# Sample attention of a hybrid decoder step: eight samples stacked in the rows of one tile, probabilities as weights

## What is computed

```python
s_c = einsum('btgrd,bngd->btgrn', q, k_cmp) * SCALE + bias    # 15 compressed blocks
p_c = masked_softmax(s_c);  o_c = einsum('btgrn,bngd->btgrd', p_c, v_cmp)
s_s = einsum('btgrd,btgkd->btgrk', q, k_sel) * SCALE + bias   # 256 cached keys (two pages) + the new one
p_s = masked_softmax(s_s);  o_s = einsum('btgrk,btgkd->btgrd', p_s, v_sel)
s_w = einsum('btgrd,bkgd->btgrk', q, kw) * SCALE + bias       # 256 keys of the window + the new one
p_w = masked_softmax(s_w);  o_w = einsum('btgrk,bkgd->btgrd', p_w, vw)
return gates[..., 0:1] * o_c + gates[..., 1:2] * o_s + gates[..., 2:3] * o_w
```

## Time and profile before

| | |
|---|---|
| median of 3 executions | 2619.27 us (2617.09 to 2621.42) |
| the profiled execution | 2622.14 us, its span 2620.4 us |
| TensorE busy | 2496.6 us, 95% of the span |
| VectorE, ScalarE, GpSimd busy | 657.9, 381.8, 132.6 us |
| mean granted TensorE clock | 0.976 |
| DMA | 326.33 MB, mean 125 GB/s |

### The profile page before, as it was taken

The page is one execution under the profiler, slowest core; times in us unless marked ns, Lnnn a source line. Parts: engine busy times, 40 slices in busy tenths (PEclk is TensorE's granted clock), DMA queues, the critical chain, the costliest instruction groups (busy, mean ns, idle before and its releaser), DMA issues.

```text
span 2620.4 us, 40309 instructions
## 1 busy us (share of the span) xinstructions
PE 2496.6 (95%) x18046; PEld 2040.0 (78%) x18046; DVE 657.9 (25%) x1320; ACT 381.8 (15%) x1039; POOL 132.6 (5%) x233
## 2 busy tenths in 40 slices
PE   8999999999989899999899999999999998999995
PEld 7887887778877678888788778878788776788884
DVE  0131321216235220111211322212342452201112
ACT  0121111121025110000201111111110241100002
POOL 0000000010110110000000000000201101100000
PEclk9999999999999989999999999999999898899998
DMA  6532332346422333444343232323554223334442
GB/s 211 177 113 89 104 101 82 123 158 208 155 87 65 110 118 127 145 144 148 109 145 128 97 99 84 112 82 114 188 180 160 65 81 112 113 119 152 142 151 81
DMA packets 86779, 326.33 MB, mean 125 GB/s; under 512 B 11808, under 2 KB 11840, under 8 KB 84432
## 3 DMA queue, kind: packets, MB, share of 16 engines
q1 hardware_dynamic: 73152, 266.44, 31.2%
q0 software_dynamic: 13456, 57.33, 6.2%
HBM read 313.29 MB, written 18.82 MB: 127 GB/s over the span
## 4 chain that ended last, share of the span: by engine, by line
PE 91%; DVE 4%; ACT 3%; issue 1%; DMA 1%; POOL 0%; DVEq 0%; ACTq 0%; SPq 0%; POOLq 0%
PE PB L500 67%; PE PB L722 2%; PE PB L838 2%; PE PB L600 2%; PE PB L610 1%; PE PB L607 1%; PE PB L470 1%; ACT ARENA L886 1%; PE PB L569 1%; PE PB L582 1%; PE PB L771 1%; PE PB L859 1%; PE PB L817 1%; ACT ARENA L1101 1%; PE PB L877 1%
## 5 line engine op out<-in xcount | busy, mean ns | idle before, releaser
L500 PE MATMUL PB<-XT,WT 128*128 128x264 f32 (+1 forms) x6016 | 1438.2, 394 | 16.4 <-DMA WT<-in_w_all 7.0
L500 PEld LDWEIGHTS PB<-XT,WT 128*128 128x128 f32 (+1 forms) x6016 | 1125.3, 191 | 233.8 <-issue 25.4
L500 PE MATMUL PB<-H,WT 128*128 128x264 f32 x2048 | 456.5, 386 | 3.1 <-DVE H L1549 3.1
L500 PEld LDWEIGHTS PB<-H,WT 128*128 128x128 f32 x2048 | 389.0, 190 | 70.2 <-issue 3.8
L886 ACT ACTIVATE ARENA<-PB 128x128 f32<-128x128 f32 (+6 forms) x213 | 93.4, 454 | 386.7 <-PE PB L600 167.3
L1546 DVE SCALAR_TENSOR_TENSOR H<-H,PB 128x264 f32<-128x264 f32 x32 | 13.7, 430 | 303.6 <-PE PB L500 303.6
L1151 DVE COPY SHO<-PB 128x9 f32<-128x9 f32 x66 | 11.0, 167 | 310.1 <-ACT H L908 258.7
L383 POOL DMA_DIRECT2D out<-in_c_win x16 | 8.1, 509 | 1389.1 <-DVE ARENA L1295 1389.1
L1117 ACT ACTIVATE ARENA<-XT 128x1056 f32<-128x1056 f32 x8 | 8.7, 1083 | 458.5 <-DVE XT L1570 458.0
L908 ACT ACTIVATE H<-PB,PD 128x264 f32<-128x264 f32 x58 | 27.8, 479 | 299.2 <-PE PB L500 299.1
L1557 DVE SCALAR_TENSOR_TENSOR XT<-PB,XT 128x264 f32<-128x264 f32 x32 | 13.8, 433 | 207.0 <-PE PB L500 207.0
(11 more groups left out here) (275 smaller groups left out, 2079.4 us busy)
## 6 DMA issues: line engine op xcount, KB each, us to landing
WT<-in_w_all SPq DMA_DIRECT2D x504, 512.0 KB, 4.7
out<-in_c_win POOLq DMA_DIRECT2D x16, 512.0 KB, 5.4
ARENA<-in_c_cmp POOLq DMA_DIRECT2D x64, 128.0 KB, 4.3
ARENA<-in_c_sel POOLq DMA_DIRECT2D x64, 128.0 KB, 2.6
ARENA<-in_c_win POOLq DMA_DIRECT2D x32, 256.0 KB, 3.4
ARENA<-in_states POOLq DMA_DIRECT2D x4, 1024.0 KB, 8.8
out<-ARENA POOLq DMA_DIRECT2D x4, 1024.0 KB, 6.1
ARENA<-in_w1d POOLq DMA_DIRECT2D x4, 1024.0 KB, 5.1
```

What stands on the lines that cost most here:

```text
L500: ins = mm(PB[0:m, bank, 0:T], WT[:, s, k, 0:m], x, start=start, stop=stop)
```

## The change

The eight samples are done at once. A tile's partitions now hold a row for each head of each sample (16 heads x 8 samples = 128). Two neighbouring samples share a strip of 32 columns of the array, and four strips make the 128: sample b = 2m + odd is in strip m. The query weights `QZ` of a sample are 32 wide with the other sample's 16 columns zero, so that both samples of a strip add into the same PSUM rows. Matmuls of neighbouring m write to PSUM partitions 32m to 32m+31.

- Scores: first the four even samples, then the four odd ones, each 16 matmuls of 128x32 weights by 257 keys and 8 by 15 keys.
- Softmax once, over 128 partitions instead of 16.
- Seven transposes of up to 128x128 instead of 56 small ones; ScalarE copies them into `PTZ`, `PCZ` and `PNT`.
- Output: the probabilities (32 columns) are now the weights and 256 columns of values stream: 2 x (16 + 4) + 8 matmuls; two transposes turn the result back, and VectorE copies it into `H`.
- Compressed keys and values are read where they lie, without copies. The gates are picked into 128 partitions with 12 matmuls instead of 3.
- Two buffers hold the keys of four samples each, and then the values of the same four. Loads: keys of the even samples behind `cm_v out` (where the first two samples' loads stood); keys of the odd ones behind prompt units 5, 6 and 7; values of each half behind the scores of that half.
- Projection matmuls: 24, 44, 8 and 6 behind the steps, 82 in place of 128; the 46 others come in `project(L, "gates")`, which now stands ahead of the wait for `zb_v out`. `TZB` is computed after the attention.

```diff
-for sample in range(NB):
-    BEHIND_MIX.update({f"sc_s{sample}": 8, f"pt_s{sample}": 6, f"o_s{sample}": 2})
+BEHIND_MIX.update({"as0": 24, "as1": 44, "as2": 8, "as3": 6})
...
+        slot = NB // 2 * 4 * KEYS
+        slots = [ARENA[:, at_att:at_att + slot], ARENA[:, 0:slot]]
+        KTS = [a.rearrange("p (m r t n) -> p m r t n", r=2, t=2, n=KEYS) for a in slots]
+        SVS = [a[:, 0:NB // 2 * 1024].rearrange("p (m i n) -> p m i n", i=4, n=256) for a in slots]
...
+                for m in range(NB // 2):
+                    load_keys(2 * m)
+
+                for m, u in ((3, UNITS - 3), (0, UNITS - 2), (1, UNITS - 1), (2, UNITS - 1)):
+                    on(po, "pv_t", L * UNITS + u, "pt1")
+                    load_keys(2 * m + 1)
+                for odd in range(2):
+                    on(po, "as_t", L, f"sc{odd}")
+                    for m in range(NB // 2):
...
+                            dma(SVS[odd][:, m, pg, :].rearrange("p (a n) -> p a n", n=P), c_sel[L, page, :, 2:4, :], d_att[odd])
+                        dma(SVS[odd][:, m, 2:4, :], c_win[L, b, :, 2:4, :], d_att[odd])
...
+                on(pe, "as_v", L, "q")
+                for odd in range(2):
+                    pe.wait_ge(d_att[odd], L * 384 + 192)
+                    for br in range(3):
                         for t in range(2):
+                            for m in range(NB // 2):
+                                b = 2 * m + odd
+                                keys = KTS[odd][:, m, br, t, :] if br < 2 else KCT[:, t, b * NBLK:b * NBLK + NBLK]
+                                ins = mm(PB[32 * m:32 * m + 32, br, 0:KEYS if br < 2 else NBLK], QZ[:, b, t, :], keys,
+                                         start=odd == 0 and t == 0, stop=odd == 1 and t == 1)
+                    mark("as_t", L, ins, f"sc{odd}")
+                    project(L, f"as{odd}")
+                on(pe, "as_v", L, "ps")
...
+                project(L, "as2")
+                on(pe, "as_a", L, "pt")
+                for odd in range(2):
+                    pe.wait_ge(d_att[odd], L * 384 + 384)
+                    for i in range(4):
+                        for m in range(NB // 2):
+                            mm(PB[32 * m:32 * m + 32, 4, 0:256], PTZ[:, i, 2 * m + odd, :], SVS[odd][:, m, i, :],
+                               start=odd == 0 and i == 0, stop=False)
...
+                project(L, "gates")
                 on(pe, "zb_v", L, "out")
                 on(pe, "gn_v", L, "out")
-                project(L, "gates")
...
+                nc.vector.memset(QZ[:, :, :, :], 0.0)
+                nc.vector.memset(PCZ[:, :, :], 0.0)
+                mark("as_v", L, nc.vector.memset(PTZ[:, :, :, :], 0.0), "zero")
```

More of the change, by code:

```diff
@@ L828, in _ @@
                 before(pe, "sc_v", (L + 1) * UNITS)
[L829 to L836, removed]
-                        for t in range(2):
[L838 to L860, removed]
-                    mark("as_t", it, ins, "o")
-                    project(L, f"o_s{b}")
@@ new lines, in _ @@
+                for br in range(2):
+                    for m in range(NB // 2):
+                        ins = mm(PB[32 * m:32 * m + 32, 4, 0:256], PNT[:, br, 32 * m:32 * m + 32],
+                                 VT[0:NB, 2, 2 * br * P:2 * br * P + 256], start=False, stop=br == 1)
+                mark("as_t", L, ins, "o")
+                project(L, "as3")
+                on(pe, "as_a", L, "os")
+                for t in range(2):
+                    ins = transpose(PB[:, 0, t * P:t * P + P], OS[:, t * P:t * P + P])
@@ L1029, in _ @@
                 on(sc, "mix_t", L, "pick")
[L1030 removed]
+                mark("mix_a", L, copy(GS.rearrange("p a b -> p (a b)"), PB[:, 5, 0:24]), "pick")
                 take_out(L, "vec")
@@ L1112, in _ @@
-                on(sc, "zb_v", L, "out")
+                take_out(L, "as0")
+                on(sc, "as_v", L, "max")
+                act(SCS[:, 0:NBLK], SCS[:, 0:NBLK], ACT.Exp, bias=NMS[:, 0:1], accum_out=RSS[:, 0:1])
+                for br in range(2):
+                    ins = act(SAS[:, br, :], SAS[:, br, :], ACT.Exp, bias=NMS[:, br + 1:br + 2], accum_out=RSS[:, br + 1:br + 2])
+                mark("as_a", L, ins, "exp")
+                take_out(L, "as1")
+                on(sc, "as_t", L, "pt")
@@ new lines, in _ @@
+                for odd in range(2):
+                    cols = slice(16 * odd, 16 * odd + 16)
+                    own_rows = lambda a: a.rearrange("p (m o h) -> p m o h", o=2, h=NH)[:, :, odd, :]
+                    for i in range(4):
+                        copy(PTZ[:, i, odd:NB:2, cols], own_rows(PB[:, 3, i * P:i * P + P]))
+                    copy(PCZ[:, odd:NB:2, cols], own_rows(PB[0:NBLK, 5, 0:P]))
+                mark("as_a", L, copy(PNT.rearrange("p a n -> p (a n)"), PB[0:NB, 5, P:3 * P]), "pt")
@@ new lines, in _ @@
+                for br in range(2):
+                    ts(SNEW[:, br, :], MASK, SAS[:, br, SEQ:KEYS], CGS[:, br + 1:br + 2], ALU.mult, ALU.mult)
+                mark("as_v", L, tt(SAS[:, :, 0:SEQ], SAS[:, :, 0:SEQ], spread(CGS[:, 1:3].unsqueeze(2), P, 2, SEQ), ALU.mult), "ps")
+                own("as_t", "tr")
+                for g in range(NG):
+                    rows = slice((g % 2) * HD, (g % 2) * HD + HD)
+                    o = PB[rows, 0, (g // 2) * P:(g // 2) * P + P].rearrange("p (b h) -> p b h", h=NH)
+                    ins = cp(hq(g), o[:, :, 4 * g:4 * g + 4].rearrange("p b r -> p r b"))
@@ L1528, in _ @@
-                before(ve, "as_v", (L + 1) * NB)
-                for g in range(NG):
-                    ins = cp(hq(g), part(OALL, g))
-                mark("aq_v", L, ins, "back")
-                own("aq_v", "back")
+                own("as_v", "back")
+                own("zb_v", "sz")
                 mark("zb_v", L, stt(H[:, ZB0:ZB0 + 8, :], H[:, Q0:Q0 + 8, :], 0.5, TZB[:, :, :], ALU.mult, ALU.mult), "out")
@@ L1631, in packed @@
     far = [bucket(SEQ - k) for k in range(KEYS)] + [bucket(SEQ - 16 * k - 31) for k in range(NBLK)]
-    out["bs"] = c(i["rel_bias"][np.array(far)].T)
+    out["bs"] = c(np.tile(i["rel_bias"][np.array(far)].T, (NB, 1)))
     s = i["state_wkv"].reshape(DEPTH, NB, NPAIR, 2, C, C)
```

157 lines of the change are left out of this document (69 added, 88 removed).

## The result

The changed kernel takes **2499.07 us** (median of 4 executions, 2496.97 to 2502.25) against 2620.35 us before (4 executions in the same job): a ratio of 0.9533, 95% interval 0.9516 to 0.9550. That is 121 us less; 2506 were forecast, with a range of 2496 to 2530. The profiled executions, 2622.14 and 2502.25 us, differ by 119.9 us.

What follows compares the result with a forecast made beforehand. TensorE, busy 95% of the span, was taken to bound the kernel. Sample attention falling from 71.8 and 76.8 to 17.6 us a layer gains 113.4 us: 2622.14 becomes 2508.7 profiled, 2506 us as median, range 2496 to 2530.

Steps and rivals of the forecast that it cites:

- two at a time: Rival for scores and outputs: a group of four matmuls costs 0.88 us, 2524 us; chance 0.17 including in-between cases.
- serial: Rival, strips one at a time: 2559 us at full clock (chance 0.06), 2633 us at the lower clock (0.01).
- Idle 3.2: TensorE's idle ahead of the first scores: 3.2 us a layer instead of 5.15, bounds 2.5 and 5.15.
- scores 5.0: Scores of a layer: 3.5 us for 257 columns plus 1.5 for 15 columns, replacing 8 times 1.94 or more.
- outputs 5.3: Outputs of a layer: 48 matmuls in 12 groups of four at 0.44 us, replacing 8 times 3.42 us.
- clock 1.5: One lower-clock penalty a layer for scores behind the remaining idle: 1.5 us, bounds 0 and 9.
- the base: Old sample attention's own time, projections priced at 0.235 us a record: 71.8 us in layer 0, 76.8 in layer 1.
- 113.4: Forecast gain in us over both layers' sample attention: (71.8 - 17.6) + (76.8 - 17.6).
- the likeliest case: Four strips side by side and loads hidden: 2506 us, reaching from 2497 to 2516; chance 0.62.
- Cost taken: 0: Loads of values and odd keys in bursts were to fit narrowly and cost nothing; late-weights rival 2514 to 2538, chance 0.13.
- The other half-clock stretches: Lower-clock stretches in the old sample stage, said to stand behind the small outputs and go with them.
- The rule on drains: Tiling-mode changes drain TensorE: with whole drains the nine seams cost 1.4 us in place of 0.9, one microsecond in all.

Runs made afterwards that it cites:

- exchanged operands: Kernel before, samples one by one, with probabilities as weights and values streaming in the outputs, transposes back left out: 2601.20 us, ratio 0.9926.
- strips apart: Changed kernel with the loop over strips moved outward, so a strip's matmuls follow each other in scores and outputs: 2526.30 us, ratio 0.9654.

## Why the prediction was right

The forecast was 7 us too high, its mechanisms held, and an error of 13 us was partly hidden by 7 us that the profiled execution lost elsewhere. That the forecast came so close is in part luck.

- **Strips.** "I take it that four also run side by side, at 0.44 us for four matmuls": 1.77 us for four groups of scores. The rivals (two at a time, serial) did not happen; the experiments show what each costs in the outputs: 9.5 us for pairs and 28.5 us for one strip at a time.
- **The terms of the new stage.** Idle 3.2 against 3.73 us (the clears took 1.86 us where 1.66 stood, the copies 2.08 where 1.9); scores 5.0 against 4.0 at full clock, since the 15-column matmuls run in strips too (0.22 us for 16 records, where 0.75 were charged); transposes 0.8 against 0.77; outputs 5.3 against 5.73, with the changes of height; clock 1.5 against 1.6 in layer 0. The "28 records with 128x128 weights" of an old output are 16; the other 12 have weights of 8 or 15 rows. With projection records at 0.2236 us (88 of them from 881.39 to 901.07) the attention's own share is 16.0 and 16.9 us, where 17.6 stood.
- **The step that was off: the base.** "0.235 us a record" came from the run behind the stage, and that run began at the lower clock. The window of the kernel before shows it:

```profile
991.83:997.50 5.67, 5.67 (x13) 0.51 0.00 0
```

  At 0.2236 us the 248 matmuls are 110.9 us, and the old stage's own share 77.4 and 82.1 us instead of 71.8 and 76.8: 10.9 us of gain were missing. Some 5.8 of them are the too high price of all 512 projection records of the two stages (0.0114 us each). The other 5 are the slow start of the gate projections itself (56.26 and 56.06 us where 240 records at 0.2236 are 53.7): it went with the change, and "their price is in both sums" left it out. The forecast had noticed the lower clock inside the stage and not that it reached past its end into the row used as the price.
- **Sum.** 113.4 + 10.9 + 2.3 for the new stage make 126.6 us, the ledger's number; the 6.9 us lost elsewhere leave 119.8. They are the lower clock of that one execution, as said above.
- **The range.** 2497 for the best case is more than its reasons give: no clock penalty (1.5) and the shortest idle (0.7 less) are 2.2 us a layer and not 4.5, so 2502. The upper end, 2516, should be 2513 by its terms. The measured 2499 lies below what these terms allow; that it is inside the likeliest case as stated, from 2497, is luck: the base was off, and the figure was wider than its terms.
- **The loads.** "Cost taken: 0" held. In the bursts the windows of the changed kernel show 231 and 259 GB/s at a busy share of 0.70 and 0.79, no projection waits for `WT` there, and the longest landing of a tile's half is 11.3 us (11.5 before). The columns are the stretch, us, busy time of TensorE, its weight loads, VectorE, ScalarE and GpSimd with their instructions, then clock, DMA share and GB/s:

```profile
869.00:880.00 11.00, 11.00 (x60) 9.01 (x62) 0.00 (x0) 0.78 (x2) 5.66 (x11) 1.00 0.70 231
882.00:893.00 11.00, 11.00 (x51) 9.41 (x50) 2.64 (x9) 1.77 (x7) 5.62 (x11) 1.00 0.79 259
```

- **The clock.** "The other half-clock stretches stood behind the small outputs, which are gone" was an assumption. The exchanged operands bear it out: nearly the same idles, and 20.5 us at the lower clock in place of 68.3. In the ledger the clock is the second largest part of the gain, 29 us.
- **The rule on drains.** One microsecond was at stake. A change of height there and back costs 0.23 us, between the 0.06 of the row cited and a whole drain of 0.16 each way. The Trainium skill ("TensorEngine Tiling (Array Packing)", Tiling Modes) says that changing the tiling mode drains TensorE. The trace of the strips apart agrees as far as starts show it: no record over 15 rows starts before the last one over 128 rows, and the first comes 0.31 us behind it (906.764 to 907.073) where neighbours of one height stand 0.22 us apart.

## What to carry to other kernels

When a matmul has few output rows, count what one column strip costs and put independent work of the same height in the other strips; the order between strips made no difference here with four records of a strip in a row, and eight in a row cost 2.7 us for each 32 records. Take the price of filler work from a stretch whose granted clock is 1.00, since a stage's lower clock can reach into the rows behind it. Look at an idle of a few microseconds for what follows it too: here removing 7.4 us of idle gave 11.4 us and removing 12.6 us more gave 20.7, so each cost half to two thirds as much again in clock, and moving filler matmuls ahead of it paid for both. It did not help where the clock fell behind short matmuls without an idle.

## What was not expected of the hardware

- TensorE starts matmuls of another strip past three waiting records of a strip (strip 1's first at 907.230 us, beside strip 0's fifth), and did not past a change from 128 rows to 15; between 15 and 8 rows it did.
- Matmuls that use 32 of 128 columns, serial for 20 us, kept the granted clock at 1.00; runs of 128-wide weights with 16 streaming columns, 3.4 us of every 14.4, did not. Once it fell behind 13.28 us without any idle, which ended in 64 records with 15 columns.
- Covering the waits around those runs left the clock of the stage at 0.91 and 0.92, while exchanging their operands and leaving the waits gave 0.97 in both layers (to the first up projection; 0.93 and 0.89 before); yet in the changed kernel an idle of 3.7 us was enough to halve it for the scores behind. Both are ways down.
